# SSD stage and mixer output in one block, first expert rows ahead of the later weights, last norm by tile

## What is computed

```python
# first block
n = rms_norm(x, norm1_w)
proj = n @ w_in                       # conv channels, gates, scalars
o_gdn = rms_norm(o_fw + o_bw, gdn_norm_w) * silu(g_gate)        # 8 heads of 128
y = (y_fw + y_bw + ssd_D * x_ssd) * silu(z)                     # SSD, 16 heads of 64
y = rms_norm(y by 2 groups of 512, ssd_norm_w)
h = x + concat([o_gdn, y]) @ w_out    # 2048 -> 1024
h = h + expert_choice_ffn(rms_norm(h, norm2_w))
x = rms_norm(h, final_norm_w)
# second block: 16 meta tokens and the 512 tokens
h = layer_norm(concat([meta, x]), emb_ln_g, emb_ln_b)
for i in range(2):
    ...                               # attention, convolution, gates, output; layer_norm
    f = swiglu(h) if i == 0 else moe_swiglu(h)    # 8 experts, top 2 of each token
    h = layer_norm(alpha * h + f, ln2_g[i], ln2_b[i])
return h[:, 16:]
```

## Time and profile before

| | |
|---|---|
| median of 3 runs | 3318.28 us (3317.02 to 3319.2) |
| the profiled execution | 3316.26 us |
| its span, first to last instruction | 3314.5 us |
| mean granted TensorE clock | 0.949 of full |
| TensorE busy | 2981.8 us, 90% |
| VectorE busy | 1054.5 us, 32% |
| ScalarE busy | 532.2 us, 16% |
| GpSimd busy | 225.7 us, 7% |
| DMA | 414.76 MB, mean 125 GB/s |

### The profile page before, as it was taken

How to read it: one execution, slowest core, us unless ns; L and a number is a source line. 1 busy time by engine, 2 the same in 40 slices (tenths; PEclk the granted TensorE clock), 3 DMA queues, 4 the chain that set the end, 5 groups by cost and what they waited for, 6 DMA issues and landing times. The chain is left out here.

```text
span 3314.5 us, 43223 instructions
## 1 busy us (share of the span) xinstructions
PE 2981.8 (90%) x18202; PEld 1815.8 (55%) x18202; DVE 1054.5 (32%) x1930; ACT 532.2 (16%) x1168; POOL 225.7 (7%) x206
## 2 busy tenths in 40 slices
PE   8998888997969969989999999999999499999894
PEld 4544775453433328867578884478775244444341
DVE  5666676452132152831310002119212211111013
ACT  3222332211011111134000000011340000000000
POOL 0001333220000000011000000000110000000000
PEclk9999898998979989999999999999999699999997
DMA  3410001106179931202011242012020715548825
GB/s 112 104 62 18 4 4 40 51 13 265 61 303 430 427 143 61 102 26 115 0 49 66 75 157 84 0 70 101 27 89 0 271 36 205 228 193 327 361 105 219
DMA packets 77873, 414.76 MB, mean 125 GB/s; under 512 B 10739, under 2 KB 12147, under 8 KB 61988
## 3 DMA queue, kind: packets, MB, share of 16 engines
q1 hardware_dynamic: 65948, 384.75, 29.3%
q10 hardware_dynamic: 8328, 15.40, 1.9%
q0 software_dynamic: 3456, 12.58, 1.0%
HBM read 383.69 MB, written 29.02 MB: 125 GB/s over the span
## 5 line engine op out<-in xcount | busy, mean ns | idle before, releaser
L3141 PE MATMUL pgu<-gu,xg 128*64 128x320 f32 (+1 forms) x2560 | 394.3, 464 | 5.6 <-POOLq L3084 4.7
L2795 PE MATMUL pp<-feat,lead 128*128 128x264 f32 x1408 | 315.5, 388 | 2.0 <-DVEq L2809 2.0
L2795 PEld LDWEIGHTS pp<-feat,lead 128*128 128x128 f32 x1408 | 269.0, 191 | 48.5 <-DVEq L2809 2.4
L3141 PEld LDWEIGHTS pgu<-gu,xg 128*64 128x64 f32 x2560 | 181.1, 138 | 204.0 <-issue 129.8
L371 PE MATMUL proj<-feat,w 128*128 128x512 f32 x576 | 256.1, 598 | 2.6 <-PEq L153 2.6
L2373 PE MATMUL ring<-feat,lead 128*128 128x264 f32 x1024 | 242.9, 399 | 3.0 <-PEq L2173 1.5
L2373 PEld LDWEIGHTS ring<-feat,lead 128*128 128x128 f32 x1024 | 199.6, 197 | 41.8 <-issue 6.8
L2373 PE MATMUL ring<-feat,w 128*128 128x264 f32 x896 | 208.7, 391 | 0.0
L3148 PE MATMUL py<-down,hm_t 128*64 128x512 f32 x880 | 200.0, 603 | 8.7 <-POOLq L3084 8.7
L2373 PEld LDWEIGHTS ring<-feat,w 128*128 128x128 f32 x896 | 170.3, 193 | 31.5 <-issue 3.1
L371 PEld LDWEIGHTS proj<-feat,w 128*128 128x128 f32 x576 | 107.4, 191 | 124.8 <-issue 124.8
(11 more groups left out here) (415 smaller groups left out, 3324.3 us busy)
## 6 DMA issues: line engine op xcount, KB each, us to landing
gu<-in_moe_gu SPq DMA_DIRECT2D x16, 3072.0 KB, 13.5
gu<-in_moe_gu SPq DMA_DIRECT2D x16, 2560.0 KB, 15.8
ring<-in_w_gate SPq DMA_DIRECT2D x16, 2048.0 KB, 13.7
ring<-in_w_up SPq DMA_DIRECT2D x16, 2048.0 KB, 15.3
ring<-in_w_down SPq DMA_DIRECT2D x16, 2048.0 KB, 17.6
w<-in_w_in SPq DMA_DIRECT2D x15, 2048.0 KB, 7.8
down<-in_moe_down SPq DMA_DIRECT2D x8, 3072.0 KB, 18.2
lead<-in_ffn_up SPq DMA_DIRECT2D x22, 1024.0 KB, 4.9
```

The source lines that it names most:

```text
L2795: last = pe.matmul(pp[:, b, a, half, 0:HALF], w[:, b, a, k * P:(k + 1) * P], core.feat[:, k, half * HALF:(half + 1) * HALF], start=k == 0, ...
L3141: last = pe.matmul(pgu[half(h), part, 0:n], xg[:, k, :], w[:, k, h, :], start=k == 0, stop=k == DK - 1)
```

## The change

The tables are issued behind the first row tile, and TensorE waits for them alone. The first gate weight piece is loaded in the block before (`GateWeights`), and the first gate tile comes ahead of `exponents(0)`; `qk` and `t64` move into free rows of `chan`. `ssd_and_gates` and `mixer_output` become one block, `ssd_and_output`: `w_out` comes in four parts of 2 MB into buffers that the SSD stage has done with; TensorE turns the o channels right behind the SSD stage, contracts them for half 0 (part 0), then turns the y channels and contracts the rest. GpSimd has no products at the second entry. ScalarE loads the first rows in `route_top_two`, and SyncE's later weight parts wait for them. The combining of the expert results and the last norm are done tile by tile in one block.

```diff
@@ enter_first_block
                 for t in range(TILES):
                     sp.dma_start(core.hid[:, t, :], A["x"][0, rows(t), :]).then_inc(rows_in[t], 16)
-                sp.dma_start(core.cst[:, :], A["shapes"]).then_inc(landed, 16)
+                    if t == 0:
+                        sp.dma_start(core.cst[:, :], A["shapes"]).then_inc(tables_in, 16)
...
-                pe.wait_ge(landed, 32)
+                pe.wait_ge(tables_in, 16)
@@ new, and called from gated_delta's SyncE list behind its table: gate_weights.load(sp, 0)
+class GateWeights:
+    RING = 3
+    KH = DK // 2
+    PIECES = 8
+    def __init__(self, core, ctx, A):
+        kept = core.sb(ctx, "gate_w", [P, self.KH, BANK])
...
+        self.buf = [kept[:, :, :], pair[:, 0, :, :], pair[:, 1, :, :]]
...
+    def load(self, sp, piece):
+        g, half = divmod(piece, 2)
+        sp.dma_start(self.buf[piece % self.RING], self.src[:, half * self.KH:(half + 1) * self.KH,
+                                                           CONV_CH + g * BANK:CONV_CH + (g + 1) * BANK]
+                     ).then_inc(self.landed[piece % self.RING], 16)
@@ gated_delta
-        qk = sb("qk", SEQ)
+        qk = core.chan[:, X0 + 7, :]
...
-        t64 = sb("t64", 2, TILES, 2 * Q)
+        t64 = core.chan[:, X0 + 6, :].rearrange("p (d t c) -> p d t c", d=2, t=TILES)
@@ ssd_and_output, SyncE behind the gate pieces
+                sp.wait_ge(exps_made, QUARTERS)
+                sp.wait_ge(s_made, STATES)
+                load_out(0, 0)
+                sp.wait_ge(gate_made, QUARTERS)
+                load_out(0, 1)
+                sp.wait_ge(xdt_made, TILES * 2 * SG)
+                sp.wait_ge(weighted, STATES)
+                sp.wait_ge(y_begun, TILES)
+                load_out(1, 1)
+                sp.wait_ge(y_made, QUARTERS)
+                load_out(1, 0)
+                sp.wait_ge(y_added, ADDS)
+                route.load(sp, A)
+                sp.wait_ge(blanked, 1)
...
@@ ssd_and_output, TensorE
+                def turn(k):
+                    if k == 0:
+                        pe.wait_ge(o_gated, 2 * TILES)
+                        pe.wait_ge(exped, QUARTERS)
+                    if k == DK:
+                        pe.wait_ge(y_scaled, TILES * SG)
+                    if k >= 2:
+                        pe.wait_ge(moved_a if k % 2 == 0 else moved_v, k // 2)
...
+                gates(0)
                 pe.wait_ge(strict_made, 2)
                 exponents(0)
...
+                for k in range(DK):
+                    turn(k)
+                all_moved(0)
+                pe.wait_ge(out_landed[0][0], 16)
...
+                for t in range(TILES):
...
+                    contract(0, 0, t)
+                for k in range(DK, MK):
+                    turn(k)
+                all_moved(1)
+                pe.wait_ge(out_landed[0][1], 16)
+                for t in range(TILES):
+                    contract(0, 1, t).then_inc(out_made, 1)
...
+                for t in range(TILES):
+                    pe.wait_ge(out_read, t + 1)
+                    contract(1, 0, t)
+                    contract(1, 1, t).then_inc(out_made, 1)
@@ ssd_and_output, ScalarE (VectorE has move(2 * n + 1) ahead of gate product n)
+                act.wait_ge(i_made, STATES)
                 for n, (t, g) in enumerate(z_order):
+                    if 2 * n < DK:
+                        move(2 * n)
                     act.wait_ge(y_gated, n + 1)
-                    act.activation(gate[:, n % 2, :], yrow(t, g), ACT.Square, accum_out=ystat[:, 0, t, g:g + 1]).then_inc(y_squared, 1)
+                    act.activation(state[:, 0, n % 2, :], yrow(t, g), ACT.Square, accum_out=ystat[:, 0, t, g:g + 1]).then_inc(y_squared, 1)
@@ enter_second_block
-                pool.wait_ge(gain_in, 16)
-                for t in range(POOLED, TILES):
-                    pool.wait_ge(squared, t + 1)
-                    h = core.hid[:, t, :]
-                    pool.tensor_tensor(h, h, g[:, :], ALU.mult).then_inc(by_pool, 1)
...
-                    if t < POOLED:
-                        dve.tensor_tensor(h, h, g[:, :], ALU.mult).then_inc(entered, 1)
-                        dve.wait_ge(entered, t + 1)
-                    else:
-                        dve.wait_ge(by_pool, t - POOLED + 1)
+                    dve.tensor_tensor(h, h, g[:, :], ALU.mult).then_inc(entered, 1)
+                    dve.wait_ge(entered, t + 1)
@@ route_top_two
                 weights.first_loads(sp)
-                sp.wait_ge(weights.scattered, 2 * TILES * 16)
+                sp.wait_ge(weights.rows_in, 32)
                 for part in range(2, PARTS):
                     weights.load(sp, 0, part)
...
                 act.activation(wt[:, 0, :], wt[:, 0, :], ACT.Exp).then_inc(exped, 1)
+                act.wait_ge(weights.scattered, 2 * TILES * 16)
+                weights.load_rows(act, 0)
@@ expert_ffn
-                act.wait_ge(weights.scattered, 2 * TILES * 16)
-                load_rows(0)
                 act.wait_ge(turned, 1)
-                load_rows(1)
+                load_rows(act, 1)
...
                 for t in range(TILES):
+                    h = core.hid[:, t, :]
                     dve.wait_ge(gathered[t], 32)
-                    h = core.hid[:, t, :]
-                    dve.scalar_tensor_tensor(out=h, in0=got[:, t, 0, :], scalar=weight[:, t, 0:1], in1=h,
-                                             op0=ALU.mult, op1=ALU.add).then_inc(enlarged, 1)
...
+                    for a in range(2):
+                        dve.scalar_tensor_tensor(out=h, in0=got[:, t, a, :], scalar=weight[:, t, a:a + 1], in1=h,
+                                                 op0=ALU.mult, op1=ALU.add).then_inc(combined, 1)
+                        dve.wait_ge(combined, 2 * t + a + 1)
+                    for half_row in range(2):
+                        norm.take_stats(dve, t, half_row)
+                    norm.normalize(dve, t)
@@ second_block
-        layer_norm(core, A, 4, ROWS[:TILES], result=result)
```

More of the change, by code:

```diff
@@ L1315, in carried, with contract, all_moved @@
                                           start=True, stop=True).then_inc(s_made, 1)
+                def turn(k):
[6 more added lines that the diff above has]
+                        pe.wait_ge(moved_a if k % 2 == 0 else moved_v, k // 2)
+                    src = core.o_acc if k < DK else core.y_acc
+                    for t in range(TILES):
+                        last = pe.transpose(turned[:, k % 2, tl(t)], src[:, t, k % DK * P:(k % DK + 1) * P], ident)
+                    last.then_inc(transposed, 1)
+                def contract(half, part, t):
+                    for k in range(part * DK, (part + 1) * DK):
+                        last = pe.matmul(out[t][:, :], mix[:, k, tl(t)], homes[half][part][:, k % DK, :], start=k == 0, stop=k == MK - 1)
+                    return last
+                def all_moved(part):
+                    pe.wait_ge(moved_a, (part + 1) * DK // 2)
+                    pe.wait_ge(moved_v, (part + 1) * DK // 2)
+                gates(0)
                 pe.wait_ge(strict_made, 2)
@@ L2160, in enter_second_block @@
     META_AT = 1
-    POOLED = 2
     with ExitStack() as ctx:
@@ L3120, in _ @@
                 act.sem_inc(all_stored, 1)
+                for t in range(TILES):
+                    norm.root(act, t)
             @block.tensor
```

296 lines of the change are left out of this document (109 added, 187 removed).

## The result

| | before | after |
|---|---|---|
| median of 5 runs | 3317.02 us (3312.91 to 3319.2) | 3290.2 us (3283.73 to 3299.51) |
| ratio of times, 95% interval | | 0.9924 [0.9905, 0.9944] |
| the profiled execution | 3316.26 us | 3290.2 us |
| its span, mean granted clock | 3314.5 us, 0.949 | 3288.4 us, 0.95 |

Faster by 26.8 us (0.8%); 3291 was forecast. The head of the profile's page shows where such a difference must be: TensorE has as much work as before (2985.5 us against 2981.8), so what went is idle time of TensorE, and time after its last matmul.

What follows compares the result with a forecast made beforehand. TensorE, busy 90% of the span, was taken to bound the kernel, with gains from removing its idleness. Terms 2.1 + 1.2 + 12.4 - 0.5 + 9.0 + 3.4 = 27.6 us gave 3291; forecast range 3284 to 3297 (0.70), overall 3284 to 3301.

Steps and rivals of the forecast that it cites:

- 1, entry: Kernel entry: identity table ahead of row tiles 1 to 3 starts the first projection 2.1 us earlier; bounds 0 and 2.6.
- 2, SSD: Head of the SSD stage: first gate tile fills a 6.6 us gap, two new waits leave 1.2 us; bounds 0 and 1.7.
- 3, joined stretch: Last SSD matmul to last contraction: turning and contracting o hides the y norm, 138.1 to 125.7 us, 12.4 less.
- 4, second entry: Entry of the second block: VectorE's first product saves 2.2 us, two more cost 1.2 each; 0.5 us lost.
- 5, first rows: Before the first expert matmul: rows asked for ahead of the later weight parts gain 9.0 us; bounds 7 and 9.6.
- 6, tail: Combine and last norm: one chain per tile, 6.9 us each, 27.6 for four, gains 3.4 us; bounds 2.4 and 4.5.
- a clock under 0.9 behind the turns: Joined SSD and output stage: a granted clock this low after the transposes was listed as showing the prediction wrong.
- Tiles 0 to 2 are turned by then: Kernel entry: when the last tile is scaled at 13.3 us, only eight transposes at 0.20 us are left.
- So of 6.6 us of gap only 1.2 are won: Head of the SSD stage: new waits, 2.4 us for weights and some 3 for mask and operand, take the rest.
- I charge nothing: Joined stage: the clock is at 2.4 GHz when the contraction starts, so no low-clock cost was counted.
- rival B: Joined stage: clock low when each contraction starts, costing 6 us in all, time 3297; chance 0.11.
- rival C: First expert unit: waits for weights or second rows replace that for first rows, losing up to 9.0 us, 3300; chance 0.10.

Runs made afterwards that it cites:

- the moves-first kernel: Changed kernel with ScalarE and VectorE moving all eight turned rows of o before gating and squaring y: 3289.75 us, ratio 0.9925; its repeat 3285.36 us.

## Why the prediction was right, point by point

The lengths of each edited stretch, over all profiles of kernels that have the part's code unedited and of those that don't:

| part | without | with | gain | forecast |
|---|---|---|---|---|
| 1, entry | 18.4 (3 profiles) | 17.5 (8; 16.6 to 18.7) | 0.9 | 2.1 |
| 2, SSD | 207.8 (3) | 207.8 (8; 205.1 to 210.7) | 0 | 1.2 |
| 3, joined stretch | 138.8 (2) | 127.4 (7; 125.7 to 128.1) | 11.4 | 12.4 |
| 4, second entry | 35.0 (3) | 35.1 (11) | 0 | -0.5 |
| 5, first rows | 22.1 (3) | 13.4 (9) | 8.7 | 9.0 |
| 6, tail | 45.9 (3) | 42.4 (11) | 3.5 | 3.4 |

The gains sum to 24.5 us, against 27.6 forecast and 26.8 and 25.4 measured by the medians of the changed kernel's two measurements. That the median fell on 3290.2 is the sum's merit to within 3 us and chance below that: the starting value of 3318.28 was 1.3 to 2.6 us above the later medians of the kernel before (3317.02 to 3315.66), and that error and the gain's partly cancelled each other. The joined stretch of 125.7 in the first profile, the forecast to the tenth, is luck too; over seven profiles it is 127.4. One sign of being wrong, a clock under 0.9 behind the turns, came up in five of the seven, and it cost about 2 us.

**The failed step, entry:** "Tiles 0 to 2 are turned by then". The time of the last scale was right, but I took the first three tiles to be turned as they came. Tile 0's scale waits for ScalarE's root, which is behind tile 1's square, and tile 1 is what the table had delayed. TensorE started 32 transposes at 9.56 and was itself the end of the chain. In the eight profiles with this part it started at 8.9 to 10.2, 9.5 on average, and in the three without at 9.5 to 9.9, 9.6 on average: the early table bought next to no earlier start. Most of the 0.9 us of the table lies in how long the 32 took, 5.1 to 6.6 us (5.5 on average) with the part and 5.6 to 6.6 (6.2) without. The profiles list a granted clock of 1.00 for all of them, so what makes that length vary stays open, and with it whether the part gains anything. The reordered roots brought the start to 7.2 to 7.4 us in three profiles; in one of them the transposes then kept pace with the tiles and the entry took 16.6 us, in the others the next row landed later and TensorE made the last 24 in one run of 5.4 us again (17.2, 18.2).

**SSD head, 1.2 us:** the waits were those forecast (2.4 to 2.8 for weights in six of eight profiles, 2.4 forecast; 2.5 to 2.7 for mask and operand in six, some 3 forecast), and `exponents(2)` came not 1.2 us nearer to the start but 1.9 to 2.7 (18.3 us behind it in six of eight profiles, 19.5 and 21.5 in the others; 20.3 to 21.0 without the part). The prediction let the chain from the end of `exponents(0)` to the operand of `exponents(2)` take the 8.2 us of before; it took 6.7 to 6.8 in six profiles. What failed is "So of 6.6 us of gap only 1.2 are won", which also counts all that follows at full clock. In two profiles of the same code, the moves-first kernel and its repeat, the matmuls behind the second wait are:

```profile
567.80 1.98 PE L1328 MATMUL pexp<-steps_and_weighted,strict 128*128 128x512 f32 x4 [0.90 <-DVE steps_and_weighted L1493]
569.62 3.60 PE L1347 MATMUL proj<-gate_w,feat 128*128 128x512 f32 x8
```

```profile
566.17 3.78 PE L1328 MATMUL pexp<-steps_and_weighted,strict 128*128 128x512 f32 x4 [0.90 <-DVE steps_and_weighted L1493]
569.75 4.75 PE L1347 MATMUL proj<-gate_w,feat 128*128 128x512 f32 x8
```

Those 12 matmuls cost 5.6 us in one and 8.5 in the other, and the stage is 205.1 and 209.8. The two shortest stages with the part (205.1 and 205.2, the clock at 1.00 in all of the stage) are some 2.5 us below those without it, the longest (210.7) 3 above; over eight profiles nothing is left. Without the part the low clock sits in the first 20 us of the stage (0.74 to 0.83) and the next 40 have 0.97 to 1.00; with it the first 20 have 0.82 to 1.00 and the next 40 still 0.92 to 1.00. That several short waits in a row give the clock more chances to fall than one long gap fits these figures, but no run tests it.

**Joined stretch:** the mechanism and its pieces were right: turns 8.5 us (8.9), second turns 6.4 (6.8), groups of 64 matmuls 27.6 (27.5), y's norm hidden. With the turns as late as before, the whole gain was lost again. The term was 1 us too large because "I charge nothing" for the clock: rival B's mechanism is real, in five of seven profiles, at the first contraction alone, and costs about 2 us there, not the 6 of its price. The Trainium skill's sentence on transposes (TensorE: Matmul & The Clock Gate, Part 4: PE-mode transpose), that the full clock "doesn't engage" for them, is contradicted once more: with each turn doubled the granted clock rose from 0.50 to 1.00 while TensorE did transposes and nothing else, and in the joined stretch of three profiles with dense turns it was never low. With the sparse turns it was low in six of seven profiles, in the turns or behind them. That points to the waits between the turns, of up to 2.0 us, as what costs the clock; three profiles against seven make it likely and don't prove it.

**Second entry:** VectorE's first product went from 3.40 us to 1.20, and the two added ones cost 1.22 each; half a microsecond either way does not show in a stretch that varies from 34.3 to 35.9. The 2.2 us did not always fall on the product. In the repeat of the kernel before, VectorE's product took 1.22 us and the centring behind it, 1.28 elsewhere, took 3.44:

```profile
1223.87 5.73 POOL L2188 TENSOR_TENSOR hid<-hid,g 128x1024 f32<-128x1024 f32 x2 [119.14 <-DMA g<-in_final_norm]
1223.88 1.22 DVE L2221 TENSOR_TENSOR hid<-hid,g 128x1024 f32<-128x1024 f32 x1
1227.24 3.44 DVE L2124 SCALAR_TENSOR_TENSOR hid<-hid,mv,gb 128x1024 f32<-128x1024 f32 x1
```

GpSimd's two products are 3.43 and 2.34 us there, the longer one beside VectorE's short product; in the first profile they are 2.33, beside VectorE's long one, and 3.32. So each time that they meet, one of the two engines is longer by about the other's instruction. This agrees with what the Trainium skill says of the port pair that the two share (SBUF — State Buffer, SBUF: two separate sides), that one of them blocks fully until the other's instruction is through.

**First rows:** 18.1 us became 9.10 between the first profiles before and after, the forecast's 9.0 in full, and 8.7 over all. The slack named for rival C is there: the changed kernel waited for nothing in the first unit, and 3.6 us less ahead of it brought a wait of 1.51 for exactly the down part.

**Tail:** the forecast chain, 27.5 us for 27.6.

**The stretches between.** They did change their length, by up to 7.4 us (gated delta), in the unchanged kernel as well; the profile of after happened to have these sum to +1.3. One profile against another can't show an edit worth less than that in such a stage; the edited stretch alone can.

## What to carry to other kernels

Where TensorE is 90% busy, an edit is worth the TensorE idle time that it removes, and it can be counted to a microsecond by following what ends the wait, what ends the next one, and what stands behind it in each list; all three large terms came out so. Where an edit replaces one long wait by several short ones, count what the clock does behind them before counting a gain. Put the work that frees the next buffer first, so that TensorE's short jobs stand close together: the moves first took 4 us off a stretch of 127.4. When the start of a unit moves ahead, its weights must move too; here 9 us were free, and of the next 3.6 the units gave back 2.2.

## What the runs showed of the hardware

The granted clock at one place differs from execution to execution of the same code: gated delta took 235.8 to 243.2 us for 5818 matmuls, at 0.92 and 0.87, and the head of the SSD stage had 1.00 and 0.85 in two profiles of one kernel (the moves first). Two loads of 128 KB took 13 us behind 11 MB of weights just issued and 3.4 us ahead of them (issued at 2596.30, turned at 2599.71 in the kernel with the weight parts in the next block), though they are on another queue. With the order undone (first rows late) it was again 12.8, issued at 2597.35 and turned at 2610.17: the order of issue decided.
